# 128 instead of 96 tokens leave the dense down product of a product-key expert layer

## The chip, the cores and the metric

The kernel is one program on one NeuronCore of a Trainium2 chip. The metric is the time of the whole program on the device, in microseconds (us). TensorE multiplies, VectorE (DVE), ScalarE (ACT) and GpSimd (POOL) do elementwise work, SyncE (SP) issues most transfers, and 16 DMA engines carry them all.

## What is computed

Two layers (DEPTH) over 512 tokens of width 1024. Each layer has a convolution and pooling mixer, and then product-key retrieval of single-neuron experts. Each token picks 128 of 16384 experts (8 heads, top 16), and the layer is, cut to what matters:

```python
idx, gate = ...                      # (512 tokens, 128 picks): expert numbers and weights of the picks
a = einsum("tmd,td->tm", u_tab[idx], x)
w = gate * gelu(a)
y = einsum("tm,tmd->td", w, v_tab[idx])      # the down product
x = x + g2 * y
```

## The kernel before

**Dense form.** Instead of gathering experts for each token the kernel multiplies all 16384 experts with all tokens. The tables are walked in 128 chunks of 128 experts (N_U = N_V = 128), four to a round (RING = 4).

- *Up stage* (`up_chunk`, `product`, L485 and L489): one chunk is 24 matmuls of 512 columns: `w_hi` times `h_hi` and `h_lo` (L485, 16), then `w_lo` times `h_hi` (L489, 8). Each f32 operand is split into a high and a low part so that three products in the reduced format add up to f32 accuracy. ACT makes `w_hi` from the loaded tile (`hi`, L651), POOL or DVE makes `w_lo`. ACT applies gelu (L765) and stores the activations to `ga_scratch` in HBM.
- *Gates*: from chunk EARLY = 64 on, LATE = 56 up chunks each also build dense gates for TOK = 8 tokens: DVE makes 8 one-hot tiles from L1289 and 16 from L1291, TensorE does 16 small matmuls (L592), ACT copies them out (L802). Blocks of 64 tokens go to `g_scratch` in HBM (7 blocks, TG = 448 tokens).
- *Down stage* (`down_chunk`, L609 and L613): one chunk loads a 512 KB tile of `v_t` (SP, L293), the activations of 448 tokens (`ga_in`, L369) and, for two chunks at a time, their gates (`g_in`, L367). DVE multiplies them (`weights`, L1337), ACT takes the high part `v_hi` (L651), DVE the low part `v_lo` (L1344) and the tile's low part `w_lo` (L1347), and TensorE does 24 matmuls of TD = 416 columns that add up in the eight PSUM banks.

**The tokens that are not in it.** The last OWN = 96 tokens take no part in the dense down product. Their picked rows of `v_t` are gathered and weighted one by one. The retrieval leaves a token per partition, so 128 picks lie beside each other in 128 partitions. To use all partitions with 96 tokens, twelve small transfers a layer (in the ACT queue) lay the picks out anew: 96 partitions hold 96 picks of a token, the 32 spare partitions the 32 others of three tokens one after the other (THIRDS = 3). That makes TURNS = 96 gathers of 128 rows (`fetch_rows`, L888, 512 KB each) and 96 gathers of 128 activations (`fetch_cells`, L897, 4 bytes each) a layer, both in POOL's queue. DVE multiplies the activations by the gates (`weigh`, L1304) and adds each row, times its weight, to one of three sums (`add`, L1311), one add behind each chunk of rounds 6 to 29. In the last chunk TensorE puts the three sums into the banks' last 96 columns, by three f32 matmuls for each k with matrices `folds`, that also turn them over (L637).

**What sets the order.** Every engine has its own instruction stream and waits on semaphores. `w_hi`, `w_lo`, `v_hi`, `v_lo` have two buffers each, so what is made for chunk n waits until the product of chunk n - 2 is done. `ring`, `ga_in` and `own_rows` have four slots. TensorE's last chunk begins only when `own_done` says that all adds are in.

## Time and profile before

| what | value |
|---|---|
| median of 3 runs | 3322.07 us (3319.07 to 3323.23) |
| the profiled execution's own time | 3322.87 us |
| its span in the profile | 3321.1 us |
| TensorE busy (matmuls) | 3237.7 us, 97% |
| TensorE weight loads | 2816.7 us, 85% |
| VectorE busy | 2482.9 us, 75% |
| ScalarE busy | 1135.9 us, 34% |
| GpSimd busy | 816.9 us, 25% |
| read from and written to HBM | 580.24 MB, 127.93 MB |

The busy share is over the whole span. Matmul ends are modelled, so that matmuls overlap in the rows, and the time that one costs is the distance between the starts of two neighbours. "PEld" is TensorE's weight load. What an engine waited for stands behind its instruction, in brackets.

### The profile page before, as it was taken

What the parts mean: (1) busy time and instruction counts of PE and PEld (TensorE: products, weight loads), DVE (VectorE), ACT (ScalarE), POOL (GpSimd) and SP (SyncE); (2) the same over time, 40 slices, a digit from 0 to 9 for tenths busy, and PEclk for the clock granted to TensorE, in tenths of its full rate; (3) what the DMA queues carried; (4) which work ended last, traced back from release to release, by engine and by line L of the source; (5) the groups of instructions that cost most, each with busy time, mean ns of one, the idle gap of its engine ahead of it and who ended that gap; (6) DMA issues with size and microseconds to landing.
All of it is one profiled execution on the core that took longest, in us unless ns stands there. A gap on an engine that the chain in (4) does not pass through costs nothing.

```text
span 3321.1 us, 56049 instructions
## 1 busy us (share of the span) xinstructions
PE 3237.7 (97%) x16466; PEld 2816.7 (85%) x16466; DVE 2482.9 (75%) x6232; ACT 1135.9 (34%) x1606; POOL 816.9 (25%) x573
## 2 busy tenths in 40 slices
PE   6989999999999999999999999999999999999998
PEld 4568888788888999999975788888888889999998
DVE  7972999779996568888677249942999945888885
ACT  3233222234443333333342332223444433333332
POOL 0033445400000134442000335443000002444420
PEclk8989999999999999999999999999999999999999
DMA  6152676445546689999721224444454567999994
GB/s 246 57 209 96 242 248 225 156 149 205 224 174 250 213 302 335 338 338 341 252 94 38 77 86 145 143 147 144 175 219 177 221 226 229 334 336 338 337 339 142
DMA packets 328417, 709.65 MB, mean 214 GB/s; under 512 B 32512, under 2 KB 180352, under 8 KB 326144
## 3 DMA queue, kind: packets, MB, share of 16 engines
q1 hardware_dynamic: 253248, 478.81, 43.1%
q10 hardware_dynamic: 41280, 128.98, 9.9%
q0 software_dynamic: 33792, 100.79, 8.0%
q8 instruction: 34, 0.56, 0.1%
q14 instruction: 63, 0.52, 0.0%
HBM read 580.24 MB, written 127.93 MB: 213 GB/s over the span
## 4 chain that ended last, share of the span: by engine, by line
PE 84%; DVE 11%; issue 4%; DMA 1%; ACT 1%; DVEq 0%; SPq 0%; ACTq 0%
PE bank L485 28%; PE bank L609 23%; PE bank L489 14%; PE bank L613 11%; PE bank L592 3%; DVE scratch L1213 2%; DVE scratch L1098 1%; PE bank L409 1%; DVE h L1194 1%; DVE h L1191 1%; PE bank L429 1%; DVE h L1193 1%; DVE h L1190 1%; DVE z_pad L1240 1%; DVE z_pad L1242 1%
## 5 line engine op out<-in xcount | busy, mean ns | idle before, releaser
L485 PE MATMUL bank<-h_hi,w_hi 128*128 128x512 f32 x2528 | 1001.3, 396 | 5.1 <-ACT scratch L651 2.3
L651 ACT ACTIVATE w_hi<-ring 128x1024 fp32r<-128x1024 f32 x584 | 615.6, 1054 | 1108.3 <-PE bank L489 1041.5
L485 PE MATMUL bank<-h_lo,w_hi 128*128 128x512 f32 x2528 | 986.3, 390 | 0.0
L609 PE MATMUL bank<-v_lo,w_hi 128*128 128x416 f32 x2032 | 711.2, 350 | 0.0
L609 PE MATMUL bank<-v_hi,w_hi 128*128 128x416 f32 x2032 | 705.1, 347 | 0.0
L874 POOL TENSOR_TENSOR w_lo<-ring,w_hi 128x1024 fp32r<-128x1024 f32 x172 | 445.7, 2592 | 859.5 <-ACT w_hi L651 859.5
L489 PE MATMUL bank<-h_hi,w_lo 128*128 128x512 f32 x2528 | 624.3, 389 | 0.0
L485 PEld LDWEIGHTS bank<-h_hi,w_hi 128*128 128x128 f32 x2528 | 475.4, 188 | 106.1 <-ACT w_hi L651 5.0
L485 PEld LDWEIGHTS bank<-h_lo,w_hi 128*128 128x128 f32 x2528 | 475.5, 188 | 98.5 <-issue 2.4
L489 PEld LDWEIGHTS bank<-h_hi,w_lo 128*128 128x128 f32 x2528 | 474.5, 188 | 98.5
L897 POOL DMA_INDIRECT h<-ga_scratch,h x192 | 182.9, 953 | 1308.0 <-DVE v_lo L1344 474.8
L1291 DVE TENSOR_SCALAR h<-iota_b,keys 128x128 f16<-128x128 f16 x1792 | 477.6, 310 | 0.0
L613 PE MATMUL bank<-v_hi,w_lo 128*128 128x416 f32 x2032 | 420.2, 348 | 0.0
L651 ACT ACTIVATE v_hi<-scratch 128x416 fp32r<-128x416 f32 x256 | 142.3, 556 | 763.0 <-PE bank L613 749.6
L1347 DVE TENSOR_TENSOR w_lo<-ring,w_hi 128x1024 fp32r<-128x1024 f32 x256 | 313.7, 1225 | 91.5 <-ACT w_hi L651 85.8
L609 PEld LDWEIGHTS bank<-v_hi,w_hi 128*128 128x128 f32 x2032 | 381.5, 188 | 0.1
L609 PEld LDWEIGHTS bank<-v_lo,w_hi 128*128 128x128 f32 x2032 | 380.0, 187 | 1.3
L613 PEld LDWEIGHTS bank<-v_hi,w_lo 128*128 128x128 f32 x2032 | 379.2, 187 | 0.6
L1344 DVE TENSOR_TENSOR v_lo<-scratch,v_hi 128x416 fp32r<-128x416 f32 x256 | 151.7, 592 | 194.1 <-ACT v_hi L651 193.9
L1289 DVE TENSOR_SCALAR h<-iota_b,keys 128x128 f16<-128x128 f16 x896 | 223.4, 249 | 0.0
L1282 DVE TENSOR_TENSOR w_lo<-ring,w_hi 128x1024 fp32r<-128x1024 f32 x112 | 137.0, 1223 | 64.2 <-ACT w_hi L651 64.1
L1337 DVE TENSOR_TENSOR scratch<-scratch 128x448 f32<-128x448 f32 x256 | 167.2, 653 | 0.0
(172 smaller groups left out, 2575.7 us busy)
## 6 DMA issues: line engine op xcount, KB each, us to landing
ring<-u_t SPq DMA_DIRECT2D x256, 512.0 KB
ring<-v_t SPq DMA_DIRECT2D x256, 512.0 KB
ga_scratch<-norm_tmp ACTq DMA_DIRECT2D x256, 256.0 KB, 2.0
g_scratch<-scratch ACTq DMA_DIRECT2D x14, 4096.0 KB, 13.7
scratch<-ga_scratch SPq DMA_DIRECT2D x256, 224.0 KB
scratch<-g_scratch SPq DMA_DIRECT2D x128, 448.0 KB
scratch<-ada_t SPq DMA_DIRECT2D x76, 512.0 KB, 5.7
ring<-wq_t SPq DMA_DIRECT2D x32, 512.0 KB
```

The lines of the kernel that those rows point to most:

```text
L485: pe.matmul(to, w_hi[:, b, k * P:(k + 1) * P], part_h[:, k, :], start=(k == 0 and part_h is h_hi), stop=False)
L489: mm = pe.matmul(to, w_lo[:, b, k * P:(k + 1) * P], h_hi[:, k, :], start=False, stop=(k == KC - 1))
L609: pe.matmul(bank[:, k, 0:TD], w_hi[:, b, k * P:(k + 1) * P], part_w[:, b, 0:TD], start=(first and part_w is v_hi), stop=False)
L613: mm = pe.matmul(bank[:, k, 0:TD], w_lo[:, b, k * P:(k + 1) * P], v_hi[:, b, 0:TD], start=False, stop=False)
L651: return act.activation(to, of, ACT.Copy)
L874: pool.tensor_tensor(w_lo[:, n % 2, :], ring[:, n % RING, :], w_hi[:, n % 2, :].bitcast(F32), ALU.subtract).then_inc(tile_used[n % RING], 1)
L897: pool.indirect_dma_start(own_w[:, n:n + 1], None, ga_cells, bass.IndirectOffsetOnAxis(ap=own_e[:, n:n + 1].bitcast(U32), axis=0))\
L1289: dve.tensor_scalar(hot2[:, b, j, :], iota_b[:, :], i2_t[:, col], None, ALU.is_equal)
L1291: ins = dve.tensor_scalar(hot1[:, b, j, q, :], iota_b[:, :], i1_t[:, col], g_part[:, col], ALU.is_equal, ALU.mult)
L1337: dve.tensor_tensor(ga, ga, g_in[:, s // 2 % 2, :, s % 2 * GTOK:(s % 2 + 1) * GTOK], ALU.mult)\
L1344: dve.tensor_tensor(v_lo[:, b, 0:TD], ga_in[:, s, 0:TD], v_hi[:, b, 0:TD].bitcast(F32), ALU.subtract)\
L1347: dve.tensor_tensor(w_lo[:, b, :], ring[:, s, :], w_hi[:, b, :].bitcast(F32), ALU.subtract)\
```

## The change

OWN becomes 128: one token per partition. The picks, gates and cell numbers stay where the retrieval made them (`own_i`, `own_e`, `own_g` are now slices of `z_flat`), and the twelve transfers that spread them are gone. TURNS becomes 128 and TD = 384. TG falls to 384 tokens as well, so there are six gate blocks and LATE = 48 up chunks with gates, and the loads of `ga_in` and `g_in` shrink from 448 to 384 tokens. There is one sum `own_y`, which the last chunk turns over with one f32 matmul of 128 columns by `ident` for each k. DVE adds one row behind each chunk of rounds 1 to 29 (116 rows), and in the last two rounds one and two in turn (12 rows), the last two of them behind the low parts of the very last chunk. POOL fetches the first three rows as soon as the picks are there, and cells run two turns ahead of rows.

```diff
@@ -75,24 +75,21 @@
 
 
     RETRIEVING = 14 * N_U // 32
-    OWN = 96
-    TD = T - OWN
+    TD = T - P
     PICKS = HEADS * TOPK
-    SPARE = P - OWN
-    THIRDS = OWN // SPARE
-    TURNS = PICKS - SPARE
+    TURNS = PICKS
     ROWS = 4
     TOK = 8
     GTOK = 64
-    GBLOCKS = -(-TD // GTOK)
-    TG = GBLOCKS * GTOK
-    EARLY, LATE = RETRIEVING + 2 * RING, TG // TOK
+    GBLOCKS = TD // GTOK
+    EARLY, LATE = RETRIEVING + 2 * RING, TD // TOK
     G_OF = [(GBLOCKS + 1) // 2, GBLOCKS // 2]
-    ADD_FIRST = 6
-    CELLS_AHEAD = 20
-    PER_THIRD = TURNS // THIRDS // ROWS
-    ADD_LAST = ADD_FIRST + TURNS // ROWS
-    assert TURNS == THIRDS * SPARE and ROWS == RING and ADD_LAST < N_V // RING
+    ADD_FIRST = 1
+    LONG_ROUNDS = 2
+    ADD_LAST = N_V // RING - LONG_ROUNDS
+    LONG_TURNS = TURNS // ROWS - (ADD_LAST - ADD_FIRST)
+    CELLS_AHEAD = 5
+    assert ROWS == RING and ROWS * LONG_TURNS * 2 == 3 * RING * LONG_ROUNDS
     GCH = GTOK // TOK
     PER_BANK = 512 // P
 
@@ -163,24 +160,22 @@
 
         g_out = part(0, 32).rearrange("p (b i t) -> p b i t", b=2, t=GTOK)
 
-        ga_in = part(0, RING)[:, 0:RING * TG].rearrange("p (s t) -> p s t", t=TG)
-        g_in = part(RING, RING)[:, 0:RING * TG].rearrange("p (s b t) -> p s b t", s=2, b=GBLOCKS)
-
-        own_y = [part(n, 2) for n in (20, 26, 28)]
-        folds = [part(22, 1)[:, n * OWN:(n + 1) * OWN] for n in range(THIRDS)]
+        ga_in = part(0, RING)[:, 0:RING * TD].rearrange("p (s t) -> p s t", t=TD)
+        g_in = part(RING, RING)[:, 0:RING * TD].rearrange("p (s b t) -> p s b t", s=2, b=GBLOCKS)
+
+        own_y = part(28, 2)
         v_rows = v_t.rearrange("l e p d -> (l e p) d")
         ga_cells = ga_dram.rearrange("e p t -> (e p t)").unsqueeze(1)
         u_flat, z_flat = (t[:, :, :].rearrange("p c t -> p (c t)") for t in (u_pad, z_pad))
         own_rows = [u_flat[:, 0:D], u_flat[:, D:2 * D], z_flat[:, 0:D], part(24, 2)]
-        picked = [z_flat[:, D + n * PICKS:D + (n + 1) * PICKS] for n in range(3)]
-
-        i1_t, i2_t, ghi_t, glo_t = (keys[:, n * T:n * T + TG] for n in range(4))
+        own_i, own_e, own_g, own_w = (z_flat[:, D + n * PICKS:D + (n + 1) * PICKS] for n in range(4))
+
+        i1_t, i2_t, ghi_t, glo_t = (keys[:, n * T:n * T + TD] for n in range(4))
         keys_v = keys[:, :].rearrange("p (s k) -> p s k", k=P)
 
         hf = h[:, :, :].rearrange("p c t -> p (c t)")
...
@@ -627,16 +622,13 @@
                 wait_hi(pe, l, r, stages["v"] + s)
                 wait_lo(pe, l, r, stages["v"] + s)
                 pe.wait_ge(w_ready, N_V * l + RING * r + (s + 1 + RING))
-                pe.wait_ge(folds_made, l + 1)
                 pe.wait_ge(own_done, l + 1)
                 for k in range(KC):
                     for w_part, v_part in ((w_hi, v_hi), (w_hi, v_lo), (w_lo, v_hi)):
                         pe.matmul(bank[:, k, 0:TD], w_part[:, b, k * P:(k + 1) * P], v_part[:, b, 0:TD],
                                   start=False, stop=(w_part is w_lo))
-                    for n in range(THIRDS):
-                        mm = pe.matmul(bank[:, k, TD:T], own_y[n][:, k * P:(k + 1) * P], folds[n],
-                                       start=(n == 0), stop=(n == THIRDS - 1))
-                    mm.then_inc(down_done, 1)
+                    pe.matmul(bank[:, k, TD:T], own_y[:, k * P:(k + 1) * P], ident[:, :], start=True, stop=True)\
+                      .then_inc(down_done, 1)
                     if k >= SUM_LAG:
                         sum_square(2 * l + 2, k - SUM_LAG)
                 pe.nop(nofuse=True).then_inc(chunk_done, 1)
@@ -778,13 +770,6 @@
                     for s in range(RING):
                         hi(r, stages["u"] + s + 2)
                         gelu(r, s)
-                act.wait_ge(own_ready, l + 1)
-                for own, of in zip((own_i, own_e, own_g), picked):
-                    act.dma_start(own[0:OWN, :], of[SPARE:P, 0:TURNS]).then_inc(own_spread, 16)
-                    for n in range(THIRDS):
-                        act.dma_start(own[OWN:P, n * SPARE:(n + 1) * SPARE], of[SPARE + n:P:THIRDS, TURNS:PICKS])\
-                           .then_inc(own_spread, 16)
-
                 def gate_block(pair, b):
 
                     for n in range(GCH):
@@ -809,7 +794,6 @@
                 with act.Fori(0, GBLOCKS // 2) as pair:
                     for b in range(2):
                         gate_block(pair, b)
-                gate_block(GBLOCKS // 2, 0)
                 with act.Fori((EARLY + LATE) // RING, N_U // RING - 1) as r:
                     for s in range(RING):
                         hi(r, stages["u"] + s + 2)
...
@@ -891,20 +874,23 @@
 
                 def fetch_cells(n):
 
-                    pool.wait_ge(w_ready, N_V * l + n + 2 + RING)
+                    if n >= CELLS_AHEAD:
+                        pool.wait_ge(w_ready, N_V * l + (n - CELLS_AHEAD + 1 + RING))
                     if n >= ROWS:
                         pool.wait_ge(cells_landed[n % ROWS], 16 * TURNS // ROWS * l + 16 * (n // ROWS))
                     pool.indirect_dma_start(own_w[:, n:n + 1], None, ga_cells,
                                             bass.IndirectOffsetOnAxis(ap=own_e[:, n:n + 1].bitcast(U32), axis=0))\
                         .then_inc(cells_landed[n % ROWS], 16)
 
+                for n in range(ROWS - 1):
+                    fetch_rows(n)
                 for s in range(RING):
                     pool.wait_ge(ga_stored[s], 16 * (N_U // RING) * l + 16 * (N_U // RING) + 16)
                 for n in range(CELLS_AHEAD):
                     fetch_cells(n)
-                for n in range(TURNS):
-                    if n + CELLS_AHEAD < TURNS:
-                        fetch_cells(n + CELLS_AHEAD)
+                for n in range(ROWS - 1, TURNS):
+                    if n + 2 < TURNS:
+                        fetch_cells(n + 2)
                     fetch_rows(n)
 
 
...
@@ -1303,12 +1289,12 @@
                     cols = bass.ds(ROWS * n, ROWS)
                     dve.tensor_tensor(own_w[:, cols], own_w[:, cols], own_g[:, cols], ALU.mult).then_inc(own_weighed, 1)
 
-                def add(n, s, to):
+                def add(n, s):
 
                     dve.wait_ge(rows_landed[s], 16 * OF_SLOT * l + 16 * n + 16)
-                    dve.wait_ge(own_weighed, WEIGHED * l + n + (THIRDS + 1))
+                    dve.wait_ge(own_weighed, WEIGHED * l + n + 2)
                     dve.wait_ge(rows_used, TURNS * l + ROWS * n + (ROWS + s))
-                    dve.scalar_tensor_tensor(to, own_rows[s], own_w[:, bass.ds(ROWS * n + s, 1)], to,
+                    dve.scalar_tensor_tensor(own_y, own_rows[s], own_w[:, bass.ds(ROWS * n + s, 1)], own_y,
                                              ALU.mult, ALU.add).then_inc(rows_used, 1)
 
                 with dve.Fori((EARLY + LATE) // RING, N_U // RING) as r:
@@ -1318,16 +1304,7 @@
                            .then_inc(tile_used[s], 1)
                 for b in range(2):
                     dve.wait_ge(g_stored[b], 16 * G_OF[b] * l + 16 * G_OF[b] + 16)
-                for to in own_y:
-                    dve.memset(to, 0.0).then_inc(own_weighed, 1)
-                for n, to in enumerate(folds):
-                    for i in range(THIRDS):
-                        every_third = slice(i, OWN, THIRDS)
-                        if i == n:
-                            ins = dve.tensor_tensor(to[:, every_third], ident[:, every_third], ident[:, OWN:P], ALU.add)
-                        else:
-                            ins = dve.tensor_copy(to[:, every_third], ident[:, every_third])
-                ins.then_inc(folds_made, 1)
+                dve.memset(own_y, 0.0).then_inc(own_weighed, 1)
 
                 def weights(r, s):
 
@@ -1360,22 +1337,28 @@
                         for s in range(RING):
                             step(r, s, own)
 
-                def late_add(to):
-                    def of(r, s):
-                        if s == 0:
-                            weigh(r - ADD_FIRST)
-                        add(r - ADD_FIRST, s, to)
-                    return of
+                def one_add(r, s):
+                    if s == 0:
+                        weigh(r - ADD_FIRST)
+                    add(r - ADD_FIRST, s)
+
+                def long_adds(r, s):
+
+                    first = 3 * (RING * (r - ADD_LAST) + s) // 2
+                    for m in range(first, first + 1 + s % 2):
+                        n = ADD_LAST - ADD_FIRST + m // ROWS + 0 * l
+                        if m % ROWS == 0:
+                            weigh(n)
+                        add(n, m % ROWS)
 
                 weights(0, 0)
                 rounds(0, ADD_FIRST, None)
-                for n, to in enumerate(own_y):
-                    rounds(ADD_FIRST + n * PER_THIRD, ADD_FIRST + (n + 1) * PER_THIRD, late_add(to))
+                rounds(ADD_FIRST, ADD_LAST, one_add)
+                for r in range(ADD_LAST, N_V // RING):
+                    for s in range(RING):
+                        step(r, s, long_adds, r == N_V // RING - 1 and s == RING - 1)
                 dve.wait_ge(rows_used, TURNS * l + TURNS + ROWS)
                 dve.nop().then_inc(own_done, 1)
-                rounds(ADD_LAST, N_V // RING - 1, None)
-                for s in range(RING):
-                    step(N_V // RING - 1, s, None, s == RING - 1)
                 for k in range(KC):
                     dve.wait_ge(down_done, KC * l + (k + 1))
                     dve.scalar_tensor_tensor(x[:, k, :], bank[:, k, :], mod[:, 5 * KC + k:5 * KC + k + 1],
```

The end of a layer on DVE. Before, the last round (rows from the fourth last chunk's `weights` on) holds no add; `x<-bank,mod,x` is the residual add behind the last chunk:

```order
L1344 TENSOR_TENSOR v_lo<-scratch,v_hi 128x416
L261 REGISTER_ALU
L1347 TENSOR_TENSOR w_lo<-ring,w_hi 128x1024
L1337 TENSOR_TENSOR scratch<-scratch 128x448
L1343 REGISTER_ALU
L1344 TENSOR_TENSOR v_lo<-scratch,v_hi 128x416
L261 REGISTER_ALU
L1347 TENSOR_TENSOR w_lo<-ring,w_hi 128x1024
L1380 ISA
L1381 SCALAR_TENSOR_TENSOR x<-bank,mod,x 128x512
```

The same place on DVE in the changed kernel (`scratch<-z_pad,scratch` and its like are the adds):

```order
L1321 TENSOR_TENSOR v_lo<-scratch,v_hi 128x384
L256 REGISTER_ALU
L1324 TENSOR_TENSOR w_lo<-ring,w_hi 128x1024
L1296 REGISTER_ALU
L1297 SCALAR_TENSOR_TENSOR scratch<-z_pad,scratch 128x1024
L1296 REGISTER_ALU
L1297 SCALAR_TENSOR_TENSOR scratch<-scratch,z_pad 128x1024
L1360 REGISTER_ALU
L1363 ISA
L1364 SCALAR_TENSOR_TENSOR x<-bank,mod,x 128x512
```

Two adds now stand between the last `w_lo` and the residual.

TensorE's last chunk, one k of eight, before (`scratch` are the three sums and the fold matrices):

```order
L634 MATMUL bank<-v_hi,w_hi 128x416
L634 MATMUL bank<-v_lo,w_hi 128x416
L634 MATMUL bank<-v_hi,w_lo 128x416
L637 MATMUL bank<-scratch 128x96 x3
L634 MATMUL bank<-v_hi,w_hi 128x416
```

And in the changed kernel:

```order
L628 MATMUL bank<-v_hi,w_hi 128x384
L628 MATMUL bank<-v_lo,w_hi 128x384
L628 MATMUL bank<-v_hi,w_lo 128x384
L630 MATMUL bank<-ident,scratch 128x128
L628 MATMUL bank<-v_hi,w_hi 128x384
```

One f32 matmul of 128 columns stands where three of 96 stood.

POOL's queue from the first gather of a layer on, before (`h<-ga_scratch,h` is a gather of activations, `u_pad<-v_t,h` and its like one of rows):

```order
L897 DMA h<-ga_scratch,h 128x1 x21
L888 DMA u_pad<-v_t,h 128x1024
L897 DMA h<-ga_scratch,h 128x1
L888 DMA u_pad<-v_t,h 128x1024
L897 DMA h<-ga_scratch,h 128x1
```

And in the changed kernel:

```order
L871 DMA u_pad<-v_t,z_pad 128x1024 x2
L871 DMA z_pad<-v_t,z_pad 128x1024
L881 DMA z_pad<-ga_scratch,z_pad 128x1 x6
L871 DMA scratch<-v_t,z_pad 128x1024
L881 DMA z_pad<-ga_scratch,z_pad 128x1
```

Three rows come ahead of all cells, and six cells ahead of the fourth row, where there were 21 ahead of the first.

## Rows read from the trace of the kernel before

**Rows 1.** The page: the span, and busy time of each engine.
```profile
span 3321.1 us, 56049 instructions
...
PE 3237.7 (97%) x16466; PEld 2816.7 (85%) x16466; DVE 2482.9 (75%) x6232; ACT 1135.9 (34%) x1606; POOL 816.9 (25%) x573
```
**Rows 2.** Busy time by stage: gates; down without rows; down with rows.
```profile
core 0: us, PE busy (x) PEld busy (x) DVE busy (x) ACT busy (x) POOL busy (x), PEclk, DMA share, GB/s
...
760.00:1040.00 280.00, 280.00 (x1734) 229.59 (x1733) 265.66 (x1092) 113.77 (x174) 0.00 (x0) 1.00 0.54 198
1095.00:1175.00 80.00, 80.00 (x430) 79.88 (x429) 41.48 (x53) 27.09 (x36) 19.23 (x19) 1.00 0.71 231
1200.00:1550.00 350.00, 350.00 (x1876) 349.45 (x1876) 284.62 (x332) 117.94 (x158) 143.64 (x151) 1.00 0.98 338
...
```
**Rows 3.** Chain of waits: start us, us, what; chunks of three kinds.
```profile
...
1041.85 3.73 PE bank L485 x16
...
1048.29 3.73 PE bank L485 x16
...
1053.83 3.63 PE bank L485 x16
...
1059.27 3.63 PE bank L485 x16
...
1091.91 2.99 PE bank L609 x16
...
1096.39 2.99 PE bank L609 x16
```
**Rows 4.** Timeline of weight loads in the last down chunk: start us, us, what.
```profile
...
1661.08 0.82 PEld L637 LDWEIGHTS bank<-scratch 128*128 128x128 f32 x6
1661.82 0.19 PEld L634 LDWEIGHTS bank<-v_hi,w_hi 128*128 128x128 f32 x1
1661.93 0.19 PEld L634 LDWEIGHTS bank<-v_lo,w_hi 128*128 128x128 f32 x1
...
```
**Rows 5.** Timeline of one down chunk with rows, the other engines.
```profile
...
1399.86 1.27 DVE L1311 SCALAR_TENSOR_TENSOR scratch<-u_pad,h,scratch 128x1024 f32<-128x1024 f32 x1
...
1401.07 0.56 ACT L651 ACTIVATE v_hi<-scratch 128x416 fp32r<-128x416 f32 x1 [2.98 <-PE bank L613]
...
1401.65 0.59 DVE L1344 TENSOR_TENSOR v_lo<-scratch,v_hi 128x416 fp32r<-128x416 f32 x1 [0.52 <-ACT v_hi L651]
...
1402.60 1.22 DVE L1347 TENSOR_TENSOR w_lo<-ring,w_hi 128x1024 fp32r<-128x1024 f32 x1 [0.36 <-ACT w_hi L651]
...
1403.75 0.68 DVE L1337 TENSOR_TENSOR scratch<-scratch 128x448 f32<-128x448 f32 x1
1403.77 0.95 POOL L888 DMA_INDIRECT u_pad<-v_t,h  x1 [0.30 <-issue]
...
1404.05 0.34 SPq L293 DMA_DIRECT2D ring<-v_t  x1
1404.35 1.27 DVE L1311 SCALAR_TENSOR_TENSOR scratch<-z_pad,h,scratch 128x1024 f32<-128x1024 f32 x1
...
```
**Rows 6.** Waits in 1250 to 1500 us (us in total, times, longest).
```profile
...
ACT v_hi L651 <- PE bank L613: 166.6, 56, 3.0
...
DVE v_lo L1344 <- ACT v_hi L651: 23.4, 55, 0.6
...
DVE scratch L1311 <- issue: 1.4, 7, 0.2
...
```
**Rows 7.** Chain of waits: last down chunk; then the score products, f32.
```profile
...
1660.87 0.56 PE bank L634 x3
1661.43 0.64 PE bank L637 x6
...
1953.10 14.57 PE bank L557 x128
...
```
**Rows 8.** The page: transfers, KB each, us from issue to landing.
```profile
...
h<-ada_t SPq DMA_DIRECT2D x20, 512.0 KB, 5.0
...
```

More of the change, by code:

```diff
@@ L182, in hybrid_encoder @@
         rest = hf[:, 3 * T:8 * T]
-        own_i, own_e, own_g, own_w = (rest[:, 1792 + n * TURNS:1792 + (n + 1) * TURNS] for n in range(4))
         vals = rest[:, 0:256].rearrange("p (s k) -> p s k", k=TOPK)
@@ L368, in load_back @@
                                      .rearrange("b p c t -> p b (c t)")).then_inc(g_landed[pair], 16)
-                    sp.dma_start(ga_in[:, slot, :], ga_dram[c][:, 0:TG]).then_inc(ga_landed[slot], 16)
+                    sp.dma_start(ga_in[:, slot, :], ga_dram[c][:, 0:TD]).then_inc(ga_landed[slot], 16)
                 load_tile(l, v_t, 0, 0, stages["v"])
@@ L881, in _ @@
                         lo(r, s)
-                pool.wait_ge(own_spread, SPREADS * l + SPREADS)
+                pool.wait_ge(own_ready, l + 1)
                 def fetch_rows(n):
```

23 lines of the change are left out of this document (11 added, 12 removed).

## The prediction

> **What bounds the kernel now.** I read the page first: TensorE is busy for 97% of the span, every other engine for less than 76% [rows 1]. The busy time by stage then shows TensorE at 50 of every 50 us in the gate stage and all through the down stage, at the full granted clock of 2.4 GHz (PEclk 1.00) [rows 2]. The chain of waits confirms it and gives the price of a chunk, as the distance between starts. A plain up chunk takes 1059.27 - 1053.83 = 5.44 us, an up chunk with gates 1048.29 - 1041.85 = 6.44 us, a down chunk 1096.39 - 1091.91 = 4.48 us [rows 3]. The list of waits shows the rest of the pipeline waiting for TensorE: ACT waited for the product before 56 of 56 `v_hi`, 3.0 us each, and no wait in that window was ended by a DMA [rows 6]. So a microsecond off TensorE's stream is a microsecond off the kernel, until the next resource is late. Two are near in the down stage with rows: the DMA engines (share 0.98, 338 GB/s) and DVE (284.62 of 350 us, 81%) [rows 2].
>
> **What a matmul costs by its columns.** An up chunk is 24 matmuls of 512 columns, 5.44 / 24 = 226.7 ns each; a down chunk is 24 of 416 columns, 186.7 ns each [rows 3]. The difference is 40.0 ns for 96 columns, 0.417 ns a column, one cycle of 2.4 GHz each; 13.3 ns are fixed. At 384 columns this gives 186.7 - 32 x 0.417 = 173.3 ns and 4.16 us a chunk. That is an extrapolation below the narrowest moving operand that this form has in the trace. Does the weight load set a floor? Its row says 0.19 us, longer than 173 ns. But in the last chunk, two loads of this same form start 0.11 us apart (1661.82 and 1661.93) [rows 4]. A load there gave way to the next after 0.11 us, so 0.19 is its length, not its pace, and the floor is at 0.11 us. I take 173.3 ns. The bounds are 186.7 (the load is the floor after all) and 173.3 (nothing says that less is possible).
>
> The Trainium skill, "Perfetto Trace Analysis", section "Identifying the Most-Contended Engine", speaks against the change: it judges TensorE's headroom by the busy share of the weight loads. That share is 349.45 of 350 us here [rows 2]; by the rule no room is left and the columns save nothing. This is the rival "loads" below.
>
> **The change part by part.**
>
> *Down chunks.* 127 chunks a layer run by this form, 2 x 127 x (4.48 - 4.16) = **-81.3 us**.
>
> *Gates.* 56 up chunks with gates become 48 a layer. Each of the 8 goes back from 6.44 to 5.44 us: 2 x 8 x 1.00 = **-16.0 us** [rows 3]. It doesn't matter whether TensorE's small matmuls or DVE's one-hot tiles (265.66 of 280 us busy there [rows 2]) set the 6.44, since both go.
>
> *Last chunk.* For each k there are now three products of 384 columns (3 x 13.3 ns less), and one f32 matmul of 128 columns for three of 96. The six passes took 0.64 us [rows 7]. The score products are f32 matmuls of 128 columns, two passes each, 14.57 us for 128 passes, 0.114 us a pass [rows 7]; two passes cost 0.23. The saving is 0.04 + 0.41 = 0.45 us, times 8 k, times 2 layers: **-7.2 us**.
>
> *The adds now end late.* This is the only new wait that I expect to show. In one chunk's frame, with t = 0 where the product two chunks earlier ends (1401.0 in rows 5), ACT's `v_hi` starts at 0.07, `v_lo` at 0.6, `w_lo` ends at 2.8, `weights` at 3.4 and the add at 4.6 [rows 5]. TensorE starts the chunk itself at t = 4.16 in the new pace. In the very last chunk no `weights` follows, but two adds of 1.27 us: `w_lo` ends at 2.8 and the adds at 5.3. The chunks with two adds before it also push DVE late. One with a single add takes 0.56 + 1.22 + 0.59 + 1.27 = 3.64 us of DVE (the 0.59 and 0.68 us of 416 and 448 columns, cut to 384), and one with two 4.91 plus a `weigh`, against 4.16; over a pair that is 8.6 for 8.3, less the 0.07 by which neighbours overlap in the rows, so the lateness stays at some 0.3 to 0.6 us. `own_done` comes at 5.3 to 5.9, and TensorE stands 1.2 to 1.8 us. The whole last chunk is queued behind that wait, and the residual, the squares and the next norm behind it, so nothing hides it: 2 x 1.5 = **+3.0 us**.
>
> *DVE elsewhere.* A steady chunk needs 3.64 us plus a quarter of a `weigh`, 3.7 of 4.16 us (88%). The next `v_lo` is due at 4.16 + 0.6 = 4.76, the add ends at about 4.5. Free, with 0.2 us to spare; and behind that `v_lo` may be 3 us late before TensorE notices (it is ready at 1.2, used at 4.16).
>
> *Transfers.* By the row a chunk with rows now moves 512 + 224 + 224 + 512 KB, 1.51 MB, which in 4.48 us is 337 GB/s, as seen [rows 2]. The new one moves 512 + 192 + 192 + 512 KB, 1.44 MB, in 4.16 us: 347 GB/s, 3% more. Rows now accompany 124 chunks a layer, not 96. Is there room? Without rows, the engines are busy for 0.71 x 4.48 = 3.18 us a chunk, with them 0.98 x 4.48 = 4.39, so a row costs 1.21 us. The tile, equally large, costs about that too; the other 1.97 us are `ga_in` and `g_in` (many small pieces), and a seventh of it goes, 0.28 us. The new sum is 4.11 us against 4.16: 99% busy. By bytes at the rate now (338 / 0.98 = 345 GB/s at full share) it is 1.44 / 0.345 = 4.18 us, and at 338 GB/s 4.27. I take the sum by parts, since it knows that the small pieces are the dear ones: no cost, with 4.27 us as the bound. A tile is issued at 1404.05 and is due at ACT's `w_hi` two products after 1405.35, 9.6 us later in the new pace; such a tile lands in 5.0 us where the engines are freer [rows 8], so a queue may grow by half before anyone waits.
>
> *Rows.* A row is issued at 1403.77 and used four adds after the one at 1399.86, at 1417.8: it landed in at most 14.0 us, since the add never waited for a DMA [rows 5, 6]. In the new order POOL issues it right behind the add that frees its slot, 1.3 us after its start, and it is due 16.6 us after that start: 15.3 us. Enough. In the last two rounds four adds pass in 2.67 chunks, 11.1 us, which leaves 9.8: between the 5.0 us of rows 8 and 14.0. I take no cost; the bound is some 4 us for the last rows, 8 in both layers. POOL needs 1.25 us an issue, 2.5 us a turn, 3.75 at one and a half turns a chunk, under 4.16.
>
> *Free edits.* The twelve small transfers, two `memset`s and nine pieces of `folds` go from ACT and DVE while TensorE works through full chunks; they hid behind it and save nothing. Rows 0 to 2 are fetched in the gate stage (DMA share 0.54 [rows 2]).
>
> **Sum.** -81.3 - 16.0 - 7.2 + 3.0 = -101.5 us. The profiled execution took 3322.87 us (1.8 over its span), which gives 3221.4; the median is 0.8 lower, 3220.6. I say **3221 us**, with its own range 3215 to 3230.
>
> **The rivals.**
>
> *Transfers set the pace* (chance 0.18). For: 0.98 share now, and less time for nearly the same bytes. Against: no one waits for a DMA at that share [rows 6]. At 4.18 us a chunk it is 2 x 124 x 0.02 = +5, 3226; at 4.27, +27, 3248. The Trainium skill, "DMA: Bandwidth & Descriptors", section "Specifications", puts HBM at about 358 GB/s for a core. An estimate by that figure is 4.03 us a chunk, below TensorE's 4.16, so by the page the chunk still fits. No run here shows 358 held over a stage; 338 is what the trace has.
>
> *Loads are the floor* (0.05). TensorE stays at 186.7 ns. Only gates, last chunk and a milder stall (1.2 x 2) change: -16.0 - 6.6 + 2.4, about 3302. For: the loads are back to back, 0.19 us long. Against: 0.11 us between two of them in rows 4, and 226.7 - 186.7 being exactly 96 cycles.
>
> *Rows come too late and adds pace the stage; slower* (0.03). An add waits for its row, DVE stands in order, and `v_lo` behind it. Its place is the four row slots: a chunk cannot be shorter than a quarter of the round trip (add, issue, landing). It decides where the chunk reaches 4.56 us (the other terms save 20 us, over 248 chunks 0.08 above 4.48), a round trip of 18.2 us and a landing of 17. The rows bound the landing at 14.0. At 20 us of round trip the chunk is 5.0 us and the kernel 3431.
>
> *The late adds cost more* (0.05): 4 us of waiting for the last rows a layer, 3229; inside the range.
>
> **The numbers.** My case has 0.69. The range runs from 3213 (no stall at the end, a little more from the gates) to 3250 (4.27 us a chunk), and leaves out the loads and the slow case. About 0.2% (6.6 us) is what can be told from no change. All cases but the slow one are faster by more: 0.97. Of the slow one's 0.03 I put 0.01 near the point where it decides, within the 0.2%, and 0.02 slower.
>
> **What would show it.** In the changed profile: 128x384 matmuls 173 ns apart and down chunks 4.16 us apart, with rows and without; 48 chunks of 6.44 us a layer, 16 plain ones behind them; in the last chunk 0.77 us a k before the first sum of squares, and TensorE's first matmul 1.2 to 1.8 us late behind the last add. Wrong would be: chunks at 4.48 with loads back to back; chunks longer with rows than without (transfers), with ACT or DVE waiting for `ring`, `ga_scratch` or rows; adds that wait for a DMA.

## The result and the profile after

The changed kernel took 3224.97 us (median of 4 runs, 3223.68 to 3226.09), the kernel before beside it 3322.65 us (4 runs): a ratio of 0.9708, 95% interval 0.9691 to 0.9725, or 97.7 us less. The prediction was 3221 us, and the time lies inside its range. The profiled execution took 3225.39 us.

The page of the changed kernel, span and busy time, to be read against [rows 1]:

```profile
span 3223.6 us, 55013 instructions
...
PE 3134.3 (97%) x16146; PEld 2716.6 (84%) x16146; DVE 2442.4 (76%) x5906; ACT 1111.4 (34%) x1574; POOL 1123.4 (35%) x701
```

TensorE lost 103 us of busy time. POOL rose from 25% to 35%, for 701 instructions after 573. That is more than the count explains; it comes up again below.

The busy time by stage in the changed kernel: the two stretches of the down stage of [rows 2], and the end of layer 1.

```profile
core 0: us, PE busy (x) PEld busy (x) DVE busy (x) ACT busy (x) POOL busy (x), PEclk, DMA share, GB/s
1095.00:1175.00 80.00, 80.00 (x464) 80.00 (x463) 66.85 (x83) 28.56 (x39) 49.99 (x40) 1.00 0.99 348
1200.00:1550.00 350.00, 350.00 (x2021) 350.00 (x2020) 293.48 (x358) 124.06 (x168) 223.87 (x169) 1.00 0.99 346
1600.00:1615.00 15.00, 10.93 (x61) 10.64 (x60) 10.66 (x13) 4.24 (x5) 3.22 (x3) 0.94 0.79 271
1615.00:1620.00 5.00, 5.00 (x19) 4.91 (x19) 2.44 (x4) 1.89 (x3) 0.00 (x0) 0.50 0.02 7
```

The first two rows are as forecast: TensorE full, DMA share 0.99, 346 GB/s (forecast 347). The last two are not: from 1600 us on TensorE is busy for 10.93 of 15 us, and then it runs at half the clock (PEclk 0.50, the level of 1.2 GHz).

The chain of waits of the changed kernel: starts of two up chunks with gates, and of two down chunks.

```profile
904.08 3.73 PE bank L480 x16
...
910.53 3.73 PE bank L480 x16
...
1085.66 2.77 PE bank L604 x16
...
1089.82 2.77 PE bank L604 x16
```

An up chunk with gates still takes 6.45 us. A down chunk takes 1089.82 - 1085.66 = 4.16 us, with rows (1200 to 1550 us) as at the start.

**The end of a layer.** The timeline of TensorE in the changed kernel around the last chunk, first of layer 1, then of layer 2 (start us, us, what, and in brackets the idle time ahead and what ended it):

```profile
1608.27 1.55 PE L608 MATMUL bank<-v_hi,w_lo 128*128 128x384 f32 x8
1613.89 0.66 PE L628 MATMUL bank<-v_hi,w_hi 128*128 128x384 f32 x1 [4.07 <-DVEq L1361]
...
3194.26 1.55 PE L608 MATMUL bank<-v_hi,w_lo 128*128 128x384 f32 x8
3197.69 0.41 PE L628 MATMUL bank<-v_hi,w_hi 128*128 128x384 f32 x1 [1.88 <-DVEq L1361]
```

Eight products take 1.39 us, so TensorE could have gone on at 1609.66 and at 3195.65. It stood for 4.2 us in layer 1 and 2.0 us in layer 2. L1361 is DVE's signal `own_done`. DVE's timeline at the end of layer 1 says why it came late:

```profile
1602.98 0.16 DVE L1290 TENSOR_TENSOR z_pad<-z_pad 128x4 f32<-128x4 f32 x1 [1.21 <-DMA z_pad<-ga_scratch,z_pad]
...
1608.28 1.28 DVE L1297 SCALAR_TENSOR_TENSOR scratch<-u_pad,z_pad,scratch 128x1024 f32<-128x1024 f32 x1 [1.66 <-DMA u_pad<-v_t,z_pad]
...
1609.95 1.22 DVE L1324 TENSOR_TENSOR w_lo<-ring,w_hi 128x1024 fp32r<-128x1024 f32 x1
1611.09 1.28 DVE L1297 SCALAR_TENSOR_TENSOR scratch<-z_pad,scratch 128x1024 f32<-128x1024 f32 x1
1612.40 1.28 DVE L1297 SCALAR_TENSOR_TENSOR scratch<-scratch,z_pad 128x1024 f32<-128x1024 f32 x1
```

The last `weigh` waited 1.21 us for its cells, the third last add 1.66 us for its row. In layer 2 the same two kinds of wait are 0.41 and 0.23 us. POOL's timeline shows that the issues themselves were late: in the last two rounds it has no pause but the 0.30 us between two issues (a cell's issue stands between each two of these rows), and three turns take 10.08 us, 3.36 us each. The chain of waits has the landing of one such row.

```profile
1589.28 1.35 POOL L871 DMA_INDIRECT z_pad<-v_t,z_pad  x1 [0.30 <-issue]
...
1599.36 1.56 POOL L871 DMA_INDIRECT u_pad<-v_t,z_pad  x1 [0.30 <-issue]
```
```profile
1601.23 8.18 DMA z_pad<-v_t,z_pad
```

Then the stand had an echo. The chain of waits of the changed kernel shows the first and the last k at the lower clock, and one behind them:

```profile
1613.89 1.30 PE bank L628 x3
1615.19 0.43 PE bank L630 x2
...
1618.39 0.96 PE bank L628 x3
1619.35 0.43 PE bank L630 x2
...
1620.86 0.53 PE bank L628 x3
1621.38 0.22 PE bank L630 x2
```

Four k took 1619.35 + 0.43 - 1613.89 = 5.9 us. At full clock a k is 0.53 + 0.22 = 0.75 us, so these cost 2.9 us more; 0.2 of it is the slower first matmul that every stand brings, also at full clock (0.76 for 0.53 us, in layer 2 too).

### The profile page after: what moved, and what is told of

The parts are those of the page before. It is cut to its first block, busy times and chain, and to the rows that moved or that the text cites. A ratio compares the mean times of both kernels' runs of the same rounds, so it can differ in the third digit from the quotient of the medians.

```text
span 3223.6 us, 55013 instructions
## 1 busy us (share of the span) xinstructions
PE 3134.3 (97%) x16146; PEld 2716.6 (84%) x16146; DVE 2442.4 (76%) x5906; ACT 1111.4 (34%) x1574; POOL 1123.4 (35%) x701
## 4 chain that ended last, share of the span: by engine, by line
PE 50%; POOL 20%; issue 16%; DVE 12%; DMA 1%; ACT 1%; DVEq 0%; POOLq 0%; SPq 0%; ACTq 0%
PE bank L480 28%; PE bank L484 14%; POOL z_pad L881 12%; POOL u_pad L871 4%; PE bank L587 3%; POOL scratch L871 2%; POOL z_pad L871 2%; DVE scratch L1199 2%; DVE scratch L1084 1%; PE bank L404 1%; DVE h L1180 1%; DVE h L1177 1%; DVE h L1179 1%; DVE h L1176 1%; DMA scratch<-ada_t 1%
## 5 line engine op out<-in xcount | busy, mean ns | idle before, releaser
L881 POOL DMA_INDIRECT z_pad<-ga_scratch,z_pad x256 | 412.1, 1610 | 886.8 <-DMA ga_scratch<-norm_tmp 809.1
L604 PE MATMUL bank<-v_hi,w_hi 128*128 128x384 f32 x2032 | 678.9, 334 | 0.0
L604 PE MATMUL bank<-v_lo,w_hi 128*128 128x384 f32 x2032 | 678.8, 334 | 0.0
L1277 DVE TENSOR_SCALAR h<-iota_b,keys 128x128 f16<-128x128 f16 x1536 | 407.8, 308 | 0.0
L608 PE MATMUL bank<-v_hi,w_lo 128*128 128x384 f32 x2032 | 393.0, 334 | 0.0
L1324 DVE TENSOR_TENSOR w_lo<-ring,w_hi 128x1024 fp32r<-128x1024 f32 x256 | 313.6, 1225 | 103.2 <-ACT w_hi L643 103.2
L643 ACT ACTIVATE v_hi<-scratch 128x384 fp32r<-128x384 f32 x256 | 134.9, 527 | 684.8 <-PE bank L608 670.7
L1321 DVE TENSOR_TENSOR v_lo<-scratch,v_hi 128x384 fp32r<-128x384 f32 x256 | 142.7, 558 | 69.6 <-ACT v_hi L643 68.4
L871 POOL DMA_INDIRECT u_pad<-v_t,z_pad x128 | 137.3, 1073 | 156.9 <-DVE scratch L1297 148.4
L1275 DVE TENSOR_SCALAR h<-iota_b,keys 128x128 f16<-128x128 f16 x768 | 190.2, 248 | 0.0
L1297 DVE SCALAR_TENSOR_TENSOR scratch<-u_pad,z_pad,scratch 128x1024 f32<-128x1024 f32 x128 | 164.0, 1282 | 10.4 <-DMA u_pad<-v_t,z_pad 1.7
```

What stands on the lines that cost most here:

```text
L604: pe.matmul(bank[:, k, 0:TD], w_hi[:, b, k * P:(k + 1) * P], part_w[:, b, 0:TD], start=(first and part_w is v_hi), stop=False)
L608: mm = pe.matmul(bank[:, k, 0:TD], w_lo[:, b, k * P:(k + 1) * P], v_hi[:, b, 0:TD], start=False, stop=False)
L643: return act.activation(to, of, ACT.Copy)
L871: pool.indirect_dma_start(own_rows[n % ROWS], None, v_rows, bass.IndirectOffsetOnAxis(ap=own_i[:, n:n + 1].bitcast(U32), axis=0))\
L881: pool.indirect_dma_start(own_w[:, n:n + 1], None, ga_cells, bass.IndirectOffsetOnAxis(ap=own_e[:, n:n + 1].bitcast(U32), axis=0))\
L1275: dve.tensor_scalar(hot2[:, b, j, :], iota_b[:, :], i2_t[:, col], None, ALU.is_equal)
```

## The experiments

The time of the kernel before, beside which these ran, was 3322.8, 3323.5 and 3323.6 us in three sets. Executions of one version spread by 2 to 10 us, so a difference between two medians of 2 or 3 us says little; the trace says more.

**e4: the columns alone.** The kernel before, with 384 columns in the down products and all else as it was; tokens 384 to 415 get no down product.

```diff
-pe.matmul(bank[:, k, 0:TD], w_hi[:, b, k * P:(k + 1) * P], part_w[:, b, 0:TD],
+pe.matmul(bank[:, k, 0:384], w_hi[:, b, k * P:(k + 1) * P], part_w[:, b, 0:384],
```

> The kernel before, with the down matmuls cut to their first 384 columns and nothing else changed (tokens 384 to 415 get no down product). All transfers, gates, adds stay as before. Theory A (columns): 4.16 us a chunk, 2 x 127 x 0.32 = 81 us less, 3241. Theory B (transfers): by the sum of busy shares this kernel needs 4.39 us of its DMA engines in each of the 96 chunks with rows, so 192 chunks of 4.39 us and some 44 us more, 3285. A result between says how far the busy share stretches.

3240.85 us (3237.64 to 3242.53), ratio 0.9749 (0.9734 to 0.9764): 82.0 us less than before, for the predicted 81.3. Its busy time by stage, in the down stage with rows:

```profile
1200.00:1550.00 350.00, 350.00 (x2021) 350.00 (x2021) 304.02 (x359) 126.38 (x168) 157.33 (x155) 1.00 1.03 363
```

It moves the loads of 448 tokens and a row in the same 4.16 us, 363 GB/s, and no chunk was longer. So the changed kernel's 346 GB/s is not at a limit, and the transfers' share, 0.98 before and 1.03 here, is no measure of one.

**e9: fewer columns still, no rows.** The version e1 (below) with 320 columns. It leaves out rows and cells, and the down product of tokens 320 to 383.

```diff
-pe.matmul(bank[:, k, 0:TD], w_hi[:, b, k * P:(k + 1) * P], part_w[:, b, 0:TD],
+pe.matmul(bank[:, k, 0:320], w_hi[:, b, k * P:(k + 1) * P], part_w[:, b, 0:320],
```

> The version without rows and cells, whose down products are now 320 columns wide, so that tokens 320 to 383 get no down product either. Theory A (a matmul costs 13.3 ns and one cycle of 2.4 GHz a column, and a load may be cut short down to 0.11 us): 146.7 ns a matmul, 3.52 us a chunk, 254 x 0.64 = 162.6 us less than without rows at 384, about 3055 us. Rival B (the weight loads, 0.19 us long and back to back, become the floor right below 173 ns): the chunk stays near 4.16 us, 3217 us. Between the two: DVE needs 0.56 + 1.22 + 0.56 = 2.3 us a chunk without adds and does not bind; the tile, activations and gates are 0.91 MB, which at 346 GB/s take 2.6 us and do not bind either.

3054.95 us (3053.53 to 3060.43), ratio 0.9199 (0.9184 to 0.9214), as theory A has it to the microsecond. The chain of waits, two neighbouring down chunks, and the busy time by stage:

```profile
1200.38 2.35 PE bank L604 x16
...
1203.90 2.35 PE bank L604 x16
```
```profile
1220.00:1350.00 130.00, 130.00 (x889) 130.00 (x888) 83.12 (x112) 54.55 (x74) 0.00 (x0) 1.00 0.82 262
```

The chunk is 3.52 us, 146.7 ns a matmul. The weight loads are busy for 130.00 of 130 us, as they were at 173 and at 187 ns. They shrink with the matmuls. Down to 320 columns the loads set no floor.

**e1: no rows.** The changed kernel without `fetch_rows`, `fetch_cells`, `weigh` and `add`: the sum stays zero, so the last 128 tokens get no down product.

```diff
-                for n in range(ROWS - 1):
-                    fetch_rows(n)
...
-                rounds(ADD_FIRST, ADD_LAST, one_add)
+                rounds(ADD_FIRST, N_V // RING - 1, None)
```

> The changed kernel without its rows: POOL fetches no rows and no cells of the last 128 tokens, DVE adds none, the sum stays zero, so those 128 tokens get no down product. Theory A (TensorE's columns set the pace of the down stage, and only the end is late through the adds): down chunks stay at 4.16 us, the last chunk starts without the 4.1 and 1.9 us of waiting and without the half clock, so some 9 us less than the changed kernel, about 3216. Theory B (the transfers, 0.99 busy with rows, set the pace): with 0.52 MB a chunk gone, chunks fall below 4.16 us, and the kernel by more than 20 us.

3217.48 us (3215.71 to 3222.81), ratio 0.9686 (0.9671 to 0.9701). All rows together cost the changed kernel 7.5 us. Its down chunks are 4.16 us too, at a DMA share of 0.71: neither DVE, POOL nor the transfers lengthen a chunk.

**e2 and e10: the adds end early.** Rounds 9 to 16 add five rows for four chunks and the rounds behind them one a chunk, so that all are in well before the end. Nothing is left out. The cells also no longer wait for DVE's progress (`w_ready`); in the changed kernel POOL's timeline shows no stop at that wait in the last rounds.

```diff
+                rounds(ADD_FIRST, FIVES_FROM, one_add)
+                with dve.Fori(0, 2) as q:
+                    for c in range(4):
+                        for s in range(RING):
+                            step(4 * q + (FIVES_FROM + c), s, five_adds(q, c))
+                rounds(FIVES_FROM + 8, N_V // RING - 1, later_add)
```

> The changed kernel with its 128 adds in rounds 1 to 30 (five a round in rounds 9 to 16, four in the others, none in the last round). Same work, other place. Theory A1 (the end waits for the adds behind the last chunk's low part): the waits of 4.1 and 1.9 us and the half clock after the first are gone, 8 to 9 us less, about 3216. Rival A2 (POOL is the bound where more than one turn falls on a chunk, 3.35 us a turn, 16.75 us for five against 16.64): about the same gain, but DVE waits for rows in rounds 9 to 16. Rival A3 (the half clock comes from somewhere else than the wait): it stays, and only some 6 us are won.

> The version whose adds end early, once more, beside the changed kernel on the same chip. If what the late adds cost is the 9 us that the trace shows (6.6 + 2.0 us and the rest), less the 2.6 us of one longer chunk near the start of each down stage that this version showed (5.38 + 4.26 for 2 x 4.16 us), it is 5 to 7 us faster than the changed kernel: 3219 us against 3225. If the late adds cost only the 3 us of the prediction, it is no faster: 3225.

> The changed kernel itself once more, on the same chip as the next one, to compare the two. Expected 3225 us, and again adds that wait for a DMA in the last two rounds of layer 1, with 2 to 4.5 us of standing for TensorE before the last chunk there.

e2 took 3219.79 us (3219.39 to 3221.87), ratio 0.9690 (0.9676 to 0.9703). Repeated on one chip with the changed kernel it took 3218.44 us (3217.46 to 3222.82), ratio 0.9692 (0.9679 to 0.9705), and the changed kernel 3226.15 us (3225.24 to 3227.60), ratio 0.9711 (0.9698 to 0.9724). No execution of the one overlaps with the other in that set; 7.7 us lie between the medians. So the late adds cost far more than 3 us, and this version is the better kernel. In neither profile does DVE wait for a row in the rounds with five adds, so rival A2 is out; e2 missed its forecast of 3216 us by 3.8. TensorE goes from the product to the last chunk there without a stand. In the first profile of it one chunk near the start of each down stage took 5.4 us instead of 4.16, behind a wait of ACT whose end the trace does not name, in the second none did; that is the part of the spread that I can point at.

**e3: cells early, adds as in the changed kernel.** POOL fetches cells two for one in turns 12 to 71, so that it has only rows to fetch at the end. As in e2, their wait for `w_ready` is gone.

```diff
-                    if n >= CELLS_AHEAD:
-                        pool.wait_ge(w_ready, N_V * l + (n - CELLS_AHEAD + 1 + RING))
...
-                    if n + 2 < TURNS:
-                        fetch_cells(n + 2)
+                    for i in range(2 if 12 <= n < 72 and n % 3 == 0 else 1):
+                        if cells < TURNS:
+                            fetch_cells(cells)
+                            cells += 1
```

> The changed kernel with the gathers of activations issued up to 22 turns ahead (two instead of one at every third turn from 12 to 72), so that POOL issues rows alone in the last 20 turns. The adds stay where they are. Theory C (of the wait at the end, 1.3 us is DVE's own work behind the last low part, the rest rows and cells that come late since POOL needs 3.35 us a turn): DVE no longer waits for a DMA in the last chunks, TensorE waits 1.2 to 1.8 us in both layers, and the clock does not fall, since 1.9 us of waiting in layer 2 did not make it fall: about 6 us less, 3219. Rival (the transfers themselves are late at 0.99 share): rows still late, waits as before, no change from 3225.

3222.64 us (3219.74 to 3226.55), ratio 0.9699 (0.9686 to 0.9712). TensorE's timeline in e3 at the end of layer 1:

```profile
1609.77 1.55 PE L608 MATMUL bank<-v_hi,w_lo 128*128 128x384 f32 x8
1612.65 0.41 PE L628 MATMUL bank<-v_hi,w_hi 128*128 128x384 f32 x1 [1.33 <-DVEq L1362]
```

The stand is 1612.65 - 1609.77 - 1.39 = 1.5 us, and the same in layer 2; no add in the last rounds waits for a DMA, and the clock stays full. This is the stand that the prediction worked out (1.2 to 1.8). What it had missed came from the cells in POOL's queue. The times alone would not show it, since e3's executions overlap with the changed kernel's. The forecast for e3 was missed by 3.6 us; one chunk of 5.4 us in each layer, as in e2's first profile, is most of it.

**e7: DVE's `w_lo` cut to one column.** POOL's instructions are as in the changed kernel. The third product uses stale values. The edit cuts `w_lo` in the up chunks with gates too, which the expectation doesn't say.

```diff
-dve.tensor_tensor(w_lo[:, b, :], ring[:, s, :], w_hi[:, b, :].bitcast(F32), ALU.subtract)
+dve.tensor_tensor(w_lo[:, b, 0:1], ring[:, s, 0:1], w_hi[:, b, 0:1].bitcast(F32), ALU.subtract)
```

> The changed kernel, except that in the down stage DVE makes only one column of w_lo (128x1 instead of 128x1024), so the third part of the product uses stale numbers. POOL's instructions and their order are the same. Theory A (an issue of POOL that begins while DVE's w_lo with its two SBUF inputs runs is held until 0.8 us behind its end): with that operation gone the cells' issues fall from 1.79 us (median) to about 0.95, the turn of POOL from 3.3 to some 2.5 us, no add waits for a DMA in the last two rounds, the adds end 1.2 us earlier in the last chunk's frame too and TensorE stands for 0 to 0.5 us there: about 3217 to 3220 us. Rival B (the issues are long because of the other transfers or their own 128 descriptors): they stay at 1.8 us, adds still wait for a DMA in the last rounds, and only the 1.2 us a layer are gained, 3222 us.

3219.93 us (3219.32 to 3222.43), ratio 0.9690 (0.9673 to 0.9706). The cells' issues by line (ns, minimum, median, maximum), in the kernel before, the changed one and e7:

```profile
L897 POOL DMA_INDIRECT h<-ga_scratch,h x192: 942/946/2002, 1096.6 to 3150.3; - x192
```
```profile
L881 POOL DMA_INDIRECT z_pad<-ga_scratch,z_pad x256: 940/1794/1807, 1085.9 to 3183.7; - x128
```
```profile
L881 POOL DMA_INDIRECT z_pad<-ga_scratch,z_pad x256: 941/1150/2008, 1087.3 to 3178.9; - x128
```

The same instruction went from 946 ns to 1794, and with DVE's operation gone to 1150. Timeline of the changed kernel, one chunk:

```profile
1119.48 0.94 POOL L871 DMA_INDIRECT u_pad<-v_t,z_pad  x1 [1.11 <-DVE scratch L1297]
...
1120.48 1.23 DVE L1324 TENSOR_TENSOR w_lo<-ring,w_hi 128x1024 fp32r<-128x1024 f32 x1 [0.39 <-ACT w_hi L643]
1120.73 1.80 POOL L881 DMA_INDIRECT z_pad<-ga_scratch,z_pad  x1 [0.30 <-issue]
```

And of the kernel before, where the cell was issued ahead of the `w_lo` that starts at 1402.60 [rows 5]:

```profile
1402.52 0.95 POOL L897 DMA_INDIRECT h<-ga_scratch,h  x1 [2.29 <-DVE v_lo L1344]
```

The issue that begins 0.25 us behind `w_lo` lasts until 0.82 us behind its end; the one that begins 0.08 us ahead of it is not touched. Theory A holds for this operation. It is not the whole: in e7 the last `weigh` found its cells in time, but the last add of layer 1 still waited 0.62 us for its row, and TensorE stood 1.1 us there (0.5 in layer 2; 0 to 0.5 were expected). The operation is not the only one that holds an issue. In the changed kernel, timeline at the start of the last two rounds:

```profile
1585.26 1.28 DVE L1297 SCALAR_TENSOR_TENSOR scratch<-z_pad,scratch 128x1024 f32<-128x1024 f32 x1
1585.40 1.96 POOL L871 DMA_INDIRECT u_pad<-v_t,z_pad  x1 [1.12 <-DVE scratch L1297]
```

A row's issue that begins 0.14 us behind an add also ends 0.82 us behind its end. The adds are still there in e7, and so are issues of rows that they hold.

**e8: a longer stand.** e3 with two more operations of 1.28 us on DVE behind the last add, whose results nobody uses.

```diff
-                dve.nop().then_inc(own_done, 1)
+                dve.scalar_tensor_tensor(own_rows[3], own_rows[2], 0.5, own_rows[2], ALU.mult, ALU.add)
+                dve.scalar_tensor_tensor(own_rows[1], own_rows[2], 0.5, own_rows[2], ALU.mult, ALU.add)\
+                   .then_inc(own_done, 1)
```

> The version with early cells (3222.6 us, TensorE stands 1.5 us before the last chunk of each layer), with two more operations of DVE of 1.28 us each behind the last add; their results are used by nobody. TensorE then stands for 1.5 + 2.56 = 4.1 us in both layers, as it did in layer 1 of the changed kernel (4.2 us), and not the 2.0 us of its layer 2. Theory A (the clock falls to 1.2 GHz after a stand of some 4 us and stays there for the first four k of the last chunk, 2.55 us more): 3222.6 + 2 x (2.56 + 2.55) = 3232.9 us. Rival B (the half clock in layer 1 had another cause, such as the load before it): only the stand, 3222.6 + 5.1 = 3227.7 us, and the first three matmuls of the last chunk in 0.53 to 0.77 us, not 0.96.

3229.64 us (3228.08 to 3230.57), ratio 0.9719 (0.9706 to 0.9733): 7.0 us over e3, between the two expectations. The trace decides between them. Its busy time by stage behind the stand of layer 1, and its chain of waits behind the stand of layer 2:

```profile
1616.00:1620.00 4.00, 4.00 (x16) 4.00 (x16) 2.25 (x3) 1.26 (x2) 0.00 (x0) 0.50 0.00 0
```
```profile
3200.09 0.76 PE bank L628 x3
3200.85 0.22 PE bank L630 x2
3201.07 0.85 PE bank L628 x3
3201.92 0.43 PE bank L630 x2
3202.34 0.96 PE bank L628 x3
```

After stands of 3.8 us in both layers the clock fell in both: 2.9 us in layer 1 and, since it fell only in the second k, 1.8 in layer 2 (the 0.2 of the first matmul included in both). Theory A, with a smaller price in one layer. Less the 1.5 us of stand and 0.2 of slower first matmul that e3 has in each layer, the trace gives 3.8 + 2.9 + 3.8 + 1.8 - 3.4 = 8.9 us over e3, and e3's two long chunks take about 2.7 of it back.

**e5: the seventh gate block.** Built and stored as before, loaded by nobody.

```diff
-    GBLOCKS = TD // GTOK
-    EARLY, LATE = RETRIEVING + 2 * RING, TD // TOK
+    GBLOCKS = TD // GTOK + 1
+    TG = GBLOCKS * GTOK
+    EARLY, LATE = RETRIEVING + 2 * RING, TG // TOK
```

> The changed kernel with the seventh gate block still built and stored, but loaded by nobody: 56 instead of 48 up chunks with gates a layer. Theory A (an up chunk with gates costs 6.447 - 5.44 = 1.01 us more than a plain one, whoever sets that pace): + 2 x 8 x 1.01 = 16.1 us, about 3241 us, and 55 distances of 6.45 us a layer in the trace. Rival B (the end of the gates is hidden, since DVE's one-hot tiles and not TensorE set the 6.44 us and the plain chunks behind them only wait for other work): less than 8 us, under 3233 us.

3246.71 us (3239.53 to 3249.91), ratio 0.9766 (0.9750 to 0.9782): 20.6 us over the changed kernel's second set, 16.1 expected, with a spread of 10 us. Rival B is out: the chunks with gates are 6.45 us apart and 8 more a layer. For the excess the trace names several pieces: the first product behind the retrieval (16 matmuls in 6.79 us), a chunk of 5.45 us near the start of layer 1's down stage, and 0.9 us before its last but one product, where a `weigh` waited 2.56 us for cells. The first of them, in the chains of waits of e5, of the kernel before and of the changed one:

```profile
598.19 6.79 PE bank L481 x16
```
```profile
597.16 5.46 PE bank L485 x16
```
```profile
596.31 3.93 PE bank L480 x16
```

It is the clock again. TensorE stands there until the next tile of `u_t` has landed and ACT is done with it, and behind the stand the kernel before shows half the clock, by stage:

```profile
598.00:600.00 2.00, 2.00 (x6) 1.52 (x6) 2.00 (x11) 1.21 (x2) 2.00 (x2) 0.50 0.58 227
```

**e6: more bytes.** e2 with activation loads of 512 tokens, of which 128 are read by nobody.

```diff
-sp.dma_start(ga_in[:, slot, :], ga_dram[c][:, 0:TD]).then_inc(ga_landed[slot], 16)
+sp.dma_start(ga_in[:, slot, :], ga_dram[c][:, 0:T]).then_inc(ga_landed[slot], 16)
```

> The version whose adds end early, with activation loads of 512 tokens instead of 384 (128 of them are read by nobody): 64 KB more in each down chunk, 1.50 MB a chunk, and 1.64 MB in rounds 9 to 16, which have five rows for four chunks. In 4.16 us these are 362 and 393 GB/s, against 346 and 376 now. Theory A (the share of the DMA engines near 1.0 is no bound, the chunk is TensorE's): the down chunks stay at 4.16 us and the time at 3220 us. Rival B (the transfers' limit lies right behind the 376 GB/s seen): rounds 9 to 16 go at 4.16 x 393 / 376 = 4.35 us a chunk, + 2 x 32 x 0.19 = 12 us, about 3232 us, with ACT or DVE waiting for a DMA.

3225.28 us (3221.11 to 3227.99), ratio 0.9709 (0.9693 to 0.9725), between the theories. Busy time by stage in the rounds with five rows, e6 and then e10:

```profile
1220.00:1350.00 130.00, 128.91 (x744) 128.59 (x743) 113.48 (x138) 45.42 (x62) 94.84 (x74) 1.00 1.04 374
```
```profile
1220.00:1350.00 130.00, 130.00 (x752) 130.00 (x751) 115.96 (x141) 46.03 (x63) 97.32 (x76) 1.00 1.04 368
```

At 368 GB/s TensorE is full. At 374 it loses 1.1 us of 130, and DVE waits for `g_scratch` (4 times, 6.6 us, between 1100 and 1600 us). So the first waits come close above 368 GB/s, and the changed kernel's 346 stays 6% below that. Whether the rate itself makes them or the longer time that each load then takes, e6 doesn't tell apart; its profiled execution is also its fastest (3221.11 us). The DMA share is 1.04 in both rows and does not tell them apart.

## Why the prediction was right, and the term that was not

**Columns.** The extrapolation to 173.3 ns and 4.16 us a chunk was right with and without rows, alone (e4: -82.0 for -81.3) and further down (e9: 146.7 ns). The argument from two loads 0.11 us apart was enough. The rule of the Trainium skill, "Perfetto Trace Analysis", section "Identifying the Most-Contended Engine", would have led astray here: the loads' busy share was 100% at 187, 173 and 147 ns.

**Gates.** 48 chunks of 6.45 us; with the eight put back, e5 loses the 16 us and 4 to 5 more that its trace puts elsewhere. **Last chunk.** 0.75 us a k for 1.20 before (0.77 was forecast).

**Transfers.** The sum by parts (4.11 of 4.16 us, 347 GB/s) met the trace (346), and the chunk kept its pace. The bounds of 4.18 and 4.27 us rested on 338 to 345 GB/s being a rate at its limit, and e4 (363) and e10 (368) show that it wasn't. The sum by parts was right with room to spare, not as a measure: by it e4 would have needed 4.39 us a chunk, and it took 4.16. The Trainium skill, "Perfetto Trace Analysis", section "Roofline", says that a single core can pull more than 358 GB/s while its neighbour is idle, up to some 120% of it; the runs agree as far as 374.

**The late adds: the term that failed.** It stood as +3.0 us. The profiled execution shows 4.2 + 2.9 us in layer 1 and 2.0 in layer 2 with 0.2 of slower start, 9.4 in all; the changed kernel's second profile shows 2.6 + 1.8 and 2.8 + 1.8, 9.0 in all, and e10 against the changed kernel is 7.7 us. The prediction's own sign against it, adds that wait for a DMA, came up in the first profile (1.66 us); in the second only the last `weigh` of each layer waited (1.3 and 1.5 us). Three steps of it:
- The stand of the bare schedule, 1.2 to 1.8 us a layer, was right (e3: 1.5).
- "POOL needs 1.25 us an issue, 2.5 us a turn, 3.75 at one and a half turns a chunk, under 4.16" was wrong. A turn is 0.94 + 0.30 + 1.80 + 0.30 = 3.3 us with one a chunk and 3.36 us in the last two rounds, and one and a half are 5.0, over 4.16. There POOL falls behind, and cells and rows land late though the way from issue to landing was short enough (8.2 us for the row shown, 9.8 allowed). The order of instructions showed the move (the cell now right behind the row, under DVE's `w_lo`); the duration was taken from rows where it stood elsewhere. That the missing price is POOL's is shown by e3; that DVE's `w_lo` makes most of it, by e7, where a turn in the last rounds takes 2.7 us (rows at 1590.82 and 1599.03, three turns), and one and a half just under 4.16.
- That a stand can cost more than itself was not in the sum. It cost 2.9 us in layer 1.

With the terms -81.3, -16.0, -7.2 alone 3322.87 would become 3218.4 us, and e10, which has no late adds, took 3218.44 (that they agree so closely is chance; e2, the same kernel, took 3219.79). With +9.4 the sum is -95.1; the profiled executions differ by 97.5. The missing 2.4 lie ahead of the change's terms, in layer 1: the first product behind the retrieval began 0.85 us earlier (596.31 for 597.16) and was 1.53 us shorter (3.93 for 5.46), since the clock had not fallen. The prediction had no term for that, and it hid a part of what the late adds cost. The long form (5.3 to 6.8 us) is in the three profiled kernels with seven gate blocks, before, e4 and e5, and the short one in all ten with six. The stands ahead of it differ too, so whether the smaller gates have a part in it is open. The rival "the late adds cost more" put 4 us of waiting for the last rows on each layer (3229). The stands were longer than 1.5 us by 2.7 and 0.5 us, in the second profile by 1.1 and 1.3, and what made them was POOL's issues, not slow transfers; the rest of the price is the clock, which it did not have.

## What to carry to other kernels

A matmul's price by its columns may be extrapolated from two widths of the same kernel, even where the weight loads are busy all the time; look for two of them closer together than their length. When work is packed denser at the end of a stage, the price of an issue must be read from where it will stand among the other engines' operations, not from where it stood. And work that gates TensorE should end a few chunks early: the wait is paid once as standing, and sometimes again as clock.
